# The opening of a two-block kernel redone: c turned first, the first norm's rms taken on token rows, two projections halved over their input rows

## The chip, the cores and the metric

One core of a Trainium2 chip runs the whole program. The metric is device time in microseconds (us); the change is judged against the kernel before. TensorE (PE) multiplies, VectorE (DVE) and ScalarE (ACT) do the elementwise work, GpSimd (POOL) helps, SyncE (SP) issues the weight transfers.

## The reference, cut to what matters

256 tokens of width 1024, f32, pass through two transformer blocks. The change touches only the start of the first:

```python
mod = jax.nn.silu(c) @ w_ada[l] + b_ada[l]              # c: 1 x 1024, w_ada: 1024 x 6144
sh1, sc1, g1, sh2, sc2, g2 = jnp.split(mod[:, None, :], N_MOD, axis=-1)
u = rmsnorm(h, norm1_w[l]) * (1.0 + sc1) + sh1
proj = u @ w_in[l]                                      # 1024 x 3584, seven parts of 512 columns
hq, hf, hi, hg, aq, ak, av = jnp.split(proj, offs, axis=-1)
o_hg = hgrn2(hq, hf, hi, hg, lower_bounds[l], hgrn_gnorm_w[l])   # gated recurrence, uses log of the forget gate of hf
...                                                     # differential attention (aq, ak, av), w_out, norm, FFN
```

Behind it stand the rest of block one, and block two (gated linear attention, retention, 32 experts), which the change leaves as they are.

## The kernel before

**Layout.** Activations are kept with features on the 128 partitions: `hT` is 8 chunks (k = 0 to 7) of 128 features x 256 tokens. x arrives in token rows (`xtok`) and is turned on PE. All small vectors arrive as rows of one tile (`prow`) through 14 transfers, are turned together and copied to `pcol`.

**Gemms.** Each f32 product is made of three fp32r products: x is split into `XH` (ACT) and `XL` (DVE), weights into a high half (ACT, `split_to`, line 872) and a low half (DVE, line 1253), in units of 128 x 1024. A unit of weights gives 24 matmuls of 256 columns (line 520); a projection of 1024 x 512 has four units. There is room for three units (`WHL`), so ACT waits for PE before the fourth. ACT and DVE split two units ahead of the gemm that they stand in.

**Weights.** SP issues pieces of 1 MB in the order of the list `order` into a ring of six slots; a slot is free again when its modulation block was summed (`ada_sum`) or its units were split. The modulation vector is computed in 12 blocks of 512 columns of `w_ada` (2 MB each). Block n gives `modc` columns 4n to 4n+3: blocks 0 and 1 the shift, 2 and 3 the scale of the first norm. A block goes through four engines' steps: `ada_sum` (16 matmuls of 512 columns, line 477), `ada_row` (ACT copy, line 947), `ada_turn` (4 products with `fold`, line 487), `modulation` (DVE, line 1295).

**Opening before.** PE: 16 transposes of x, the transpose of `prow`, the column sums of the squares (`norm_sums`, line 464, on the turned x, squared by ACT), then blocks 0, 1, 2, 3 one after another, 8 spin matmuls, and gemm hf, gemm hq. DVE: reciprocal of `rstd`, normalised x, then per chunk x times scale plus shift and `XL`. Behind gemm hf stands the forget gate: ACT sigmoid, DVE steps (1692 to 1697), ACT Ln (1121), DVE scan (1700). DVE and ACT split no weights in between, beyond the two units ahead. Then a `weave` runs aq, ak, av, hv, hg and wo0 on all engines, with the recurrence (`gated`), blocks 4 to 9 and attention (`diff`) in lanes between gemm steps. Every engine works its instructions in the written order.

Of the kernel before, what the change touches and what calls it, by code (L numbers as in the profile page):

```python
# [14 lines left out]
P = 128  # L15
# [23 lines left out]
            subln=97, gkb=98, glan=102, retn=104, c=120)  # L39
# [55 lines left out]
def build(nc, a, out):  # L95
    ctx = ExitStack()
    with ctx:
# [55 lines left out]
        xtok = early.take([P, TT, D])  # L153
        scratch = Region(ARENA - 1024 - KC * T).take([P, KC, T])
        mrow = [Region(ARENA - 1024 + 512 * i).take([P, 512]) for i in range(2)]
        xmod = Region(P).take([P, KC, T])
# [145 lines left out]
        G = [Gemm("hf", win(1), 0), Gemm("hq", win(0), 0), Gemm("aq", win(4), 0), Gemm("ak", win(5), 0),  # L302
# [49 lines left out]
        order = (["ada0", "ada1", "ada2", "ada3", "hf", "hq", "aq", "ada4", "ada5", "ak", "ada6", "ada7", "av",  # L352
# [30 lines left out]
        def x_last(idx):  # L383
# [17 lines left out]
        S.xT, S.hT_a, S.hT_v = sem("xT"), sem("hT_by_act"), sem("hT_by_dve")  # L401
        S.ada_p, S.ada_a, S.mod, S.xn = (sem(n) for n in ("ada_pe", "ada_act", "ada_mod", "x_normed"))
        S.sqrt_table, S.sq, S.sqw, S.ss, S.rms, S.rstd, S.nrm = (sem("norm_" + n) for n in (
            "table", "squares", "weighed_squares", "sums", "rms", "rstd", "scaled"))
        S.scl, S.lb_v, S.lb_a, S.lam_v, S.lam_a, S.lam_p, S.chain = (sem(n) for n in (
            "scl", "bounds_dve", "bounds_act", "lambda_dve", "lambda_act", "lambda_pe", "chain"))
# [37 lines left out]
        def tensor(e):  # L444
# [24 lines left out]
            def ada_sum(n):  # L469

                b = 6 + n % 2
                clear(b)
                w.wait_ge(S.cT, 1)
                for r in range(2):
                    w.wait_ge(*landed(f"ada{n}", r))
                    for q in range(4):
                        ins = e.matmul(bank[b][32 * q:32 * q + 32, :], c32[:, 4 * r + q, :],
                                       in_slot(f"ada{n}", r, 4, 512)[:, q, :], start=r == 0, stop=r == 1)
                ins.then_inc(S.ada_p, 1)

            def ada_turn(n):

                b = 6 + n % 2
                w.wait_ge(S.consts, 5)
                w.wait_ge(S.ada_a, n + 1)
                for c in range(4):
                    ins = e.matmul(bank[b][:, c:c + 1], mrow[n % 2][:, c * P:(c + 1) * P], fold[:, :], start=True,
                                   stop=True)
                ins.then_inc(S.ada_p, 1)
                free[b] = (S.mod, n + 1)  # L490
# [128 lines left out]
            def third_sums(ks):  # L619
                for k in ks:  # L620
                    for i, x in enumerate((scratch, sq2)):
                        if k == 0:
                            clear(4 + i)
                        w.wait_ge(S.sqw if i else S.sq, k + 1 if i else 2 * KC + k + 1)
# [75 lines left out]
            w.wait_ge(S.d_ident, 16)  # L700
            w.wait_ge(S.d_x, 16)
            for k in range(KC):
                b = 4 + k % 4
                clear(b)
                for j in range(TT):
                    ins = e.transpose(bank[b][:, j * P:(j + 1) * P], xtok[:, j, k * P:(k + 1) * P], ident[:, :])
                ins.then_inc(S.xT, 1)
                free[b] = (S.hT_v if k % 2 else S.hT_a, k // 2 + 1)
            w.wait_ge(S.d_rows, 14 * 16)
            e.transpose(bank[0][:, 0:P], prow, ident[:, :]).then_inc(S.rows_T, 1)  # L710
            free[0] = (S.pcol, 1)
            norm_sums(0)
            for n in range(4):
                ada_sum(n)
                if n == 1:
                    clear(5)
                    w.wait_ge(S.lam_v, 4)
                    e.matmul(bank[5][:, 0:1], ones[0:1, :], lams[0:1, 5:6], start=True, stop=True).then_inc(S.lam_p, 1)
                    free[5] = (S.lam_v, 5)
                ada_turn(n)  # L720
            spin(3, 8)


            run(gemm("hf"))
            run(gemm("hq"))
            weave([gemm(n) for n in ("aq", "ak", "av", "hv", "hg", "wo0")],
                  (0, ada(ada_sum, range(4, 10))),
                  (-1, gated(HG, [(S.hb, 1), by["hq"].freed[1]], by["hv"].freed[1])),
                  (0, ada(ada_turn, range(4, 10))), (4, diff()))
            run(gemm("wo1"))  # L730
            norm_sums(1)
# [129 lines left out]
        def scalar(e):  # L861
# [79 lines left out]
            def norm_split(i, base, shift):  # L941
                for k in range(KC):
                    split_x(base + k, k, scratch[:, k, :], (S.nrm, KC * (i - 1) + k + 1), modc[:, shift + k:shift + k + 1])

            def ada_row(n):
                w.wait_ge(S.ada_p, 2 * n + 1)
                e.activation(mrow[n % 2], bank[6 + n % 2][:, :], ACT.Copy).then_inc(S.ada_a, 1)
# [146 lines left out]
            for dst_, src in row_loads(True):  # L1094
                e.dma_start(dst_, src).then_inc(S.d_rows, 16)
            for k in range(0, KC, 2):
                w.wait_ge(S.xT, k + 1)
                e.activation(hT[:, k, :], bank[4 + k % 4][:, 0:T], ACT.Copy).then_inc(S.hT_a, 1)
            w.wait_ge(S.pcol, 1)
            e.activation(c32[:, :, :], pcol[:, ROWS["c"]:ROWS["c"] + 8].unsqueeze(2).broadcast_to([P, KC, 32]),  # L1100
                         ACT.Silu).then_inc(S.cT, 1)
            norm_rms(0, lambda k: (S.hT_v if k % 2 else S.hT_a, k // 2 + 1))
            ada_row(0)
            w.wait_ge(S.lb_v, 3)
            e.activation(small[:, 20:28], small[:, 20:28], ACT.Exp).then_inc(S.lb_a, 1)
            w.wait_ge(S.lam_v, 2)
            e.activation(lams[:, 2:4], lams[:, 0:2], ACT.Exp).then_inc(S.lam_a, 1)
            for n in range(1, 4):
                ada_row(n)
            w.wait_ge(S.scl, 1)  # L1110
            w.wait_ge(S.xn, 2)
            for k in range(KC):
                e.activation(XH[:, k, :], scratch[:, k, :], ACT.Identity, bias=modc[:, k:k + 1],
                             scale=scl[:, k:k + 1]).then_inc(S.x_hi, 1)
                if k == 0:
                    split_to(2)


            run(gemm("hf", to_features(hf, func=ACT.Sigmoid)))
            w.wait_ge(S.gate_v, 6)  # L1120
            e.activation(hf, hf, ACT.Ln).then_inc(S.gate_a, 1)
            run(gemm("hq", to_features(hq)))
# [7 lines left out]
            norm_rms(1, lambda k: (S.res, k + 1))  # L1130
            norm_split(1, 16, 24)
# [12 lines left out]
            w.wait_ge(S.ss, 3)  # L1144
# [98 lines left out]
        def vector(e):  # L1243
# [38 lines left out]
            def norm_apply(i, base, weight, shift):  # L1282
                w.wait_ge(S.rstd, i + 1)
                w.wait_ge(S.scl, i + 1)
# [8 lines left out]
            def modulation(n):  # L1293
                w.wait_ge(S.ada_p, 2 * n + 2)
                e.tensor_tensor(modc[:, 4 * n:4 * n + 4], bank[6 + n % 2][:, 0:4], pcol[:, 4 * n:4 * n + 4],
                                ALU.add).then_inc(S.mod, 1)
# [340 lines left out]
            w.wait_ge(S.d_lam, 64)  # L1637
            e.tensor_tensor(lamrow[:, 0::2, :], lamrow[:, 0::2, :], lamrow[:, 1::2, :], ALU.mult).then_inc(S.lam_v, 1)
            w.wait_ge(S.lam_v, 1)
            e.tensor_reduce(lams[:, 0:2], lamrow[:, 0::2, :], AXX, ALU.add).then_inc(S.lam_v, 1)  # L1640
            for k in range(1, KC, 2):
                w.wait_ge(S.xT, k + 1)
                e.tensor_copy(hT[:, k, :], bank[4 + k % 4][:, 0:T]).then_inc(S.hT_v, 1)
            w.wait_ge(S.rows_T, 1)
            e.tensor_copy(pcol[:, :], bank[0][:, 0:P]).then_inc(S.pcol, 1)
# [5 lines left out]
            norm_rstd(0)  # L1651
            w.wait_ge(S.rstd, 1)
# [594 lines left out]
```

## Time and profile before

| | us |
|---|---|
| time, median of 3 runs | 1380.79 (1374.78 to 1382.4) |
| the profiled execution, its own time | 1377.91 |
| its span | 1376.1 |
| PE busy | 1290.4 |
| DVE busy | 605.0 |
| ACT busy | 470.5 |

The span is what the profiler saw of the execution; 1.8 us lie around it. PE is the engine that is nearly always at work, so what counts is when it waits, and for whom.

### The profile page before, as it was taken

Reading aid. Unit: us, or ns where it says so; the run is one execution under the profiler, and the core shown is the slowest. Engines: PE = TensorE matmul, PEld = TensorE weight load, DVE = VectorE, ACT = ScalarE, POOL = GpSimd, SP = SyncE. Lnnn points to the kernel's source line nnn. Section 1 sums busy time; section 2 is a strip of 40 time slices with the busy share of each in tenths; the row PEclk is TensorE's granted clock in tenths of the full one; section 3 lists DMA queues with packets and bytes.
Section 4 is the critical chain, followed back from the end, with each engine's and each line's share of the span. In section 5 each row is a group of like instructions: output and inputs, shape, how many; then the busy total and the mean of one; then the engine's idle time right before and its main releaser. Section 6 shows DMA issues by size and latency. Waiting matters only on the chain. (4 is left out here: it accounts for less than half of the span.)

```text
span 1376.1 us, 18603 instructions
## 1 busy us (share of the span) xinstructions
PE 1290.4 (94%) x8067; PEld 958.5 (70%) x8067; DVE 605.0 (44%) x925; ACT 470.5 (34%) x688; POOL 60.9 (4%) x57
## 2 busy tenths in 40 slices
PE   6898869999999999799999999889999999999996
PEld 3886758999998989679999999644344443434432
DVE  2776667344556586485755556431110111101112
ACT  3643545433444644444554454211000000000001
POOL 2021000000000121010020000000000000000000
PEclk9999979999999999899999999999999999999999
DMA  9776313675544434344355545859999999999993
GB/s 353 268 264 241 125 59 123 217 243 184 184 138 153 157 125 161 107 157 150 123 161 185 184 162 179 356 242 401 422 421 421 421 420 421 421 421 421 421 421 136
DMA packets 102163, 349.86 MB, mean 254 GB/s; under 512 B 5856, under 2 KB 9216, under 8 KB 77504
## 3 DMA queue, kind: packets, MB, share of 16 engines
q1 hardware_dynamic: 100624, 345.56, 66.4%
q0 software_dynamic: 1168, 2.99, 0.7%
q8 instruction: 65, 1.06, 0.3%
q14 instruction: 18, 0.15, 0.0%
q10 hardware_dynamic: 288, 0.10, 0.0%
HBM read 347.57 MB, written 1.05 MB: 253 GB/s over the span
## 5 line engine op out<-in xcount | busy, mean ns | idle before, releaser
L520 PE MATMUL bank<-XH,WHL 128*128 128x256 f32 x2928 | 544.2, 286 | 16.2 <-DVE WHL L1253 8.6
L520 PEld LDWEIGHTS bank<-XH,WHL 128*128 128x128 f32 x2928 | 464.6, 194 | 22.9 <-issue 10.7
L520 PE MATMUL bank<-XL,WHL 128*128 128x256 f32 x1464 | 416.5, 285 | 0.0
L1253 DVE TENSOR_TENSOR WHL<-weights,WHL 128x1024 fp32r<-128x1024 f32 x223 | 279.7, 1270 | 209.6 <-ACT WHL L872 209.1
L872 ACT ACTIVATE WHL<-weights 128x1024 fp32r<-128x1024 f32 x223 | 231.8, 1054 | 210.4 <-PE bank L520 210.2
L520 PEld LDWEIGHTS bank<-XL,WHL 128*128 128x128 f32 x1464 | 283.9, 194 | 0.2
L520 PE MATMUL bank<-WHL,XH 128*128 128x512 f32 x320 | 106.0, 406 | 9.4 <-DVE WHL L1253 9.4
L1921 DVE TENSOR_TENSOR chainm<-bank,chainm 128x512 f32<-128x512 f32 x16 | 11.1, 692 | 171.9 <-PE bank L818 171.9
L818 PE MATMUL bank<-weights,arena 128*64 128x512 f32 x384 | 84.5, 592 | 0.0
L818 PE MATMUL bank<-arena 128*64 128x512 f32 x384 | 84.4, 592 | 0.0
L520 PEld LDWEIGHTS bank<-WHL,XH 128*128 128x128 f32 x320 | 62.4, 195 | 26.2 <-DVE WHL L1253 11.7
L1929 DVE COPY yo<-bank 128x512 f32<-128x512 f32 x16 | 11.1, 692 | 144.4 <-PE bank L853 144.4
L818 PEld LDWEIGHTS bank<-arena 128*64 128x64 f32 x384 | 27.6, 137 | 54.8 <-issue 54.8
L818 PEld LDWEIGHTS bank<-weights,arena 128*64 128x64 f32 x384 | 27.5, 137 | 54.6 <-issue 54.6
L520 PE MATMUL bank<-WHL,XL 128*128 128x512 f32 x160 | 64.2, 401 | 0.0
L696 PE MATMUL bank<-yo,arena 128*128 128x512 f32 x128 | 57.7, 593 | 0.8 <-DVE yo L1929 0.8
L683 PE MATMUL bank<-arena 128*128 128x256 f32 x256 | 56.9, 379 | 1.6 <-DVE arena L1615 1.6
L818 PE MATMUL bank<-late_weights,arena 128*64 128x512 f32 x256 | 56.3, 592 | 0.0
L683 PEld LDWEIGHTS bank<-arena 128*128 128x128 f32 x256 | 48.0, 190 | 8.3 <-DVE arena L1615 1.8
L1239 ACT ACTIVATE yo<-bank 128x512 f32<-128x512 f32 x16 | 9.6, 597 | 123.9 <-PE bank L853 123.9
L853 PE MATMUL bank<-arena,masks 128*64 128x512 f32 x192 | 44.5, 614 | 2.7 <-ACT masks L1233 2.7
L853 PE MATMUL bank<-weights,masks 128*64 128x512 f32 x192 | 43.0, 596 | 2.7 <-ACT masks L1233 2.7
(313 smaller groups left out, 1137.6 us busy)
## 6 DMA issues: line engine op xcount, KB each, us to landing
weights<-in_w_in SPq DMA_DIRECT2D x58, 1024.0 KB, 5.0
weights<-in_w_ada SPq DMA_DIRECT2D x24, 1024.0 KB, 7.4
weights<-in_expert_w_gate SPq DMA_DIRECT2D x24, 1024.0 KB, 14.7
weights<-in_expert_w_up SPq DMA_DIRECT2D x24, 1024.0 KB, 16.0
arena<-in_expert_w_up SPq DMA_DIRECT2D x24, 1024.0 KB, 18.5
arena<-in_expert_w_down SPq DMA_DIRECT2D x24, 1024.0 KB, 20.6
weights<-in_expert_w_down SPq DMA_DIRECT2D x24, 1024.0 KB, 21.0
arena<-in_expert_w_gate SPq DMA_DIRECT2D x24, 1024.0 KB, 16.6
```

The costliest lines, as they stand in the source:

```text
L520: ins = e.matmul(o, l, r, start=first, skip_group_check=True, stop=g.part == g.parts - 1 and k == g.kc - 1 and n == 2)
L683: ins = e.matmul(bank[b][:, kk * T:(kk + 1) * T], utok[:, j, k * P:(k + 1) * P], pick[:, j, :], start=j == 0, stop=j == TT - 1)
L696: e.matmul(bank[b][:, :], wpT[p % 2][:, j * P:(j + 1) * P], yo[p % 2][:, n * 512:(n + 1) * 512], start=p == 0, stop=p == NPAIR - 1, skip_g ...
L818: ins = e.matmul(bank[b][64 * s_:64 * s_ + 64, :], xg[:, k, p % 2 * P + 64 * s_:p % 2 * P + 64 * s_ + 64], moe_weights(x, 4, HID)[:, kk, : ...
L853: ins = e.matmul(bank[6 + n][64 * s_:64 * s_ + 64, :], hpT[p % 2][:, k, 64 * s_:64 * s_ + 64], moe_weights(x, 2, D)[:, kk, n * 512:(n + 1) ...
L872: e.activation(unit_halves(U)[0], unit_weights(g, u), ACT.Copy).then_inc(S.w_hi, 1)
L1239: e.activation(yo[p % 2][:, 512:1024], bank[7][:, :], ACT.Copy).then_inc(S.m_ya, 1)
L1253: e.tensor_tensor(lo, unit_weights(g, u), hi, ALU.subtract).then_inc(S.w_lo, 1)
L1921: e.tensor_tensor(hp[p % 2], bank[5][:, :], hp[p % 2], ALU.mult).then_inc(S.m_h2, 1)
L1929: e.tensor_copy(yo[p % 2][:, 0:512], bank[6][:, :]).then_inc(S.m_yv, 1)
```

## The change

1. SP loads c into a tile of its own (`crow`), then x, then b_ada. c is turned alone, first on PE; its silu on ACT no longer waits for `pcol`.
2. Of the other row transfers, two stay on ACT's queue and ten go from ACT's queue to POOL's, behind the four lambda transfers and ahead of `masks`. PE waits for all of them before it turns `prow`.
3. x is turned in four groups of one token block and four chunks; DVE makes all four copies to `hT`.
4. The rms is taken on token rows: ACT squares `xtok` with a sum along the row (2 instructions), square root, DVE reciprocal; DVE multiplies `ident` by it (2 tiles, `diag`), PE multiplies by `ones`, and ACT copies the result to `rstd`. The 8 squares, the column sums and the 128x256 reciprocal go.
5. Modulation blocks come in the order 0, 2, 1, 3. The first two give shift and scale of chunks 0 to 3.
6. hf and hq become hf0, hf1, hq0, hq1, each over half of the input rows (k = 0 to 3, k = 4 to 7, two units each), adding up in the same banks. The order is hf0, hq0 on chunks 0 to 3 (block 1's sum inside hq0, block 3 behind it), then hf1, hq1.
7. Normalising is one DVE instruction per chunk; the shift goes into `XH` and `XL`.

```diff
+        half = lambda name, i, part: Gemm(f"{name}{part}", win(i)[part * 512:(part + 1) * 512, :], 0, kc=4, parts=2, part=part,
+                                          xo=4 * part)
+        G = [half("hf", 1, 0), half("hq", 0, 0), half("hf", 1, 1), half("hq", 0, 1), Gemm("aq", win(4), 0), Gemm("ak", win(5), 0),
...
-        order = (["ada0", "ada1", "ada2", "ada3", "hf", "hq", "aq", "ada4", "ada5", "ak", "ada6", "ada7", "av",
+        ADA = [0, 2, 1] + list(range(3, 12))
+        order = (["ada0", "ada2", "hf0", "hq0", "ada1", "ada3", "hf1", "hq1", "aq", "ada4", "ada5", "ak", "ada6", "ada7", "av",
...
# PE
+            w.wait_ge(S.d_ident, 32)
+            e.transpose(bank[2][:, 0:KC], crow, ident[0:KC, 0:KC]).then_inc(S.rows_T, 1)
...
+            w.wait_ge(S.d_rows, 3 * 16)
+            w.wait_ge(S.d_lam, 14 * 16)
+            e.transpose(bank[0][:, 0:NROWS], prow[0:NROWS, :], ident[0:NROWS, 0:NROWS]).then_inc(S.rows_T, 1)
...
+            for j in range(TT):
+                w.wait_ge(S.x_v, 2 + j)
+                ins = e.matmul(bank[1][:, j * P:(j + 1) * P], ones[:, :], diag[:, j, :], start=True, stop=True)
...
-            norm_sums(0)
-            for n in range(4):
-                ada_sum(n)
...
-            spin(3, 8)
-            run(gemm("hf"))
-            run(gemm("hq"))
+            for i in range(2):
+                ada_sum(i)
+                ada_turn(i)
...
+            spin(0, 4)
+            run(gemm("hf0"))
+            hq0 = gemm("hq0")
+            next(hq0)
+            ada_sum(2)
+            run(hq0)
+            ada_turn(2)
+            ada_sum(3)
+            ada_turn(3)
+            spin(4, 10)
+            run(gemm("hf1"))
+            run(gemm("hq1"))
...
# ACT
+            for j in range(TT):
+                w.wait_ge(S.d_x, 16)
+                e.activation(xsq[:, j, :], xtok[:, j, :], ACT.Square, accum_out=small[:, 44 + j:45 + j]).then_inc(S.x_a, 1)
...
+            def first_split(half):
+                for k in range(4 * half, 4 * half + 4):
+                    split_x(k, k, scratch[:, k, :], (S.nrm, k + 1), modc[:, k:k + 1])
+                    if k == 0:
+                        split_to(2)
+            first_split(0)
+            split_to(4)
+            ada_row(2)
+            ada_row(3)
+            first_split(1)
+            run(gemm("hf1", to_features(hf, func=ACT.Sigmoid)))
...
# DVE
+            def first_norm(half):
+                ks = slice(8 + 4 * half, 12 + 4 * half)
+                w.wait_ge(S.mod, 2 * half + 2)
...
+                for k in range(4 * half, 4 * half + 5):
+                    if k < 4 * half + 4:
...
+                        e.scalar_tensor_tensor(out=scratch[:, k, :], in0=hT[:, k, :], scalar=scl[:, k:k + 1],
+                                               in1=rstd[:, :], op0=ALU.mult, op1=ALU.mult).then_inc(S.nrm, 1)
+                    if k > 4 * half:
+                        split_x(k - 1, k - 1, scratch[:, k - 1, :], modc[:, k - 1:k])
+                        if k == 1:
+                            split_to(1)
+            first_norm(0)
+            split_to(3)
+            w.wait_ge(S.lam_p, 1)
+            e.tensor_copy(neglam, bank[3][:, 0:1]).then_inc(S.lam_v, 1)
+            split_to(4)
+            modulation(2)
+            modulation(3)
+            first_norm(1)
+            run(gemm("hf1"))
...
# POOL, behind the four lambda transfers
+            for dst_, src in row_loads("pool"):
+                e.dma_start(dst_, src).then_inc(S.d_lam, 16)
...
# which queue a row goes to
-                if (name not in ("c", "b_ada")) == on_act:
+                if {"b_ada": "sp", "norm1": "act", "norm2": "act"}.get(name, "pool") == queue:
```

The order on the engines shows what the lists and calls come to. First PE from its start to its first fp32r product, before (L706 turns x, L710 `prow`, L464 the sums of squares, L477 sums and L487 turns a modulation block, L457 spins, L520 is gemm hf):

```order
-L706 MATMUL bank<-ident,arena 128x128 x16
-L710 MATMUL bank<-ident,arena 128x128
-L464 MATMUL bank<-arena,ones 128x256 x8
-L477 MATMUL bank<-weights,c 32x512 x8
-L487 MATMUL bank<-fold,arena 128x1 x4
-L477 MATMUL bank<-weights,c 32x512 x8
-L718 MATMUL bank<-lams,ones 128x1
-L487 MATMUL bank<-fold,arena 128x1 x4
-L477 MATMUL bank<-weights,c 32x512 x8
-L487 MATMUL bank<-fold,arena 128x1 x4
-L477 MATMUL bank<-weights,c 32x512 x8
-L487 MATMUL bank<-fold,arena 128x1 x4
```

And the same place of the change (L709 turns c, L716 x, L722 `prow`, L727 spreads the reciprocal rms, L485 sums and L495 turns a block, L465 spins, L528 is gemm hf0):

```order
+L709 MATMUL bank<-ident,arena 128x8
+L716 MATMUL bank<-ident,arena 128x128 x16
+L722 MATMUL bank<-ident,arena 128x120
+L727 MATMUL bank<-r,ones 128x128 x2
+L485 MATMUL bank<-weights,c 32x512 x8
+L495 MATMUL bank<-fold,arena 128x1 x4
+L485 MATMUL bank<-weights,c 32x512 x8
+L495 MATMUL bank<-fold,arena 128x1 x4
+L734 MATMUL bank<-lams,ones 128x1
+L465 MATMUL bank<-ident 128x128 x4
+L528 MATMUL bank<-XH,WHL 128x256
```

Two blocks instead of four now stand ahead of the first gemm product, and the sums of squares are gone from PE. The second place is DVE from the first block's half to the forget gate, in the change (L1718 normalises a chunk, L1306 writes `XL`, L1284 writes the low half of a unit of weights, L1327 is `modulation`, L1710 `scl`):

```order
+L1284 TENSOR_TENSOR WHL<-weights,WHL 128x1024 x2
+L1727 COPY small<-bank 128x1
+L1284 TENSOR_TENSOR WHL<-weights,WHL 128x1024
+L1327 TENSOR_TENSOR modc<-bank,pcol 128x4 x2
+L1710 SCALAR_TENSOR_TENSOR scl<-modc,pcol 128x4
+L1718 SCALAR_TENSOR_TENSOR arena<-hT,scl,rstd 128x256 x2
+L1306 SCALAR_TENSOR_TENSOR XL<-arena,modc,XH 128x256
+L1718 SCALAR_TENSOR_TENSOR arena<-hT,scl,rstd 128x256
+L1306 SCALAR_TENSOR_TENSOR XL<-arena,modc,XH 128x256
+L1718 SCALAR_TENSOR_TENSOR arena<-hT,scl,rstd 128x256
+L1306 SCALAR_TENSOR_TENSOR XL<-arena,modc,XH 128x256 x2
+L1284 TENSOR_TENSOR WHL<-weights,WHL 128x1024 x4
```

Before, one group of eight chunks stood there with two units of weights split behind the first chunk; now the units of hf1 (the last row) are split behind all four chunks of the second half. The third place is SP's queue, in the change, where pieces of `w_ada` (L2087) and of `w_in` (L2078) now take turns:

```order
+L2067 DMA arena<-in_c 8x128
+L2068 DMA arena<-in_x 128x2x1024
+L2070 DMA arena<-in_b_ada 48x128
+L2087 DMA weights<-in_w_ada 128x4x512 x4
+L2078 DMA weights<-in_w_in 128x4x512 x2
+L2087 DMA weights<-in_w_ada 128x4x512 x4
+L2078 DMA weights<-in_w_in 128x4x512 x4
+L2087 DMA weights<-in_w_ada 128x4x512 x4
```

Before, eight pieces of `w_ada` stood ahead of six of `w_in`; the pieces are as many and as large as before.

## Rows read from the trace of the kernel before

**Rows 1.** Timeline of PE's opening (start, us busy, engine, line, operation, idle before)

```profile
6.84 2.37 PE L706 MATMUL bank<-ident,arena 128*128 128x128 f32 x10 [6.84 <-DMA arena<-in_x]
...
10.86 0.39 PE L710 MATMUL bank<-ident,arena 128*128 128x128 f32 x1
...
14.73 5.23 PE L464 MATMUL bank<-arena,ones 128*128 128x256 f32 x16 [3.49 <-ACT arena L930]
...
19.90 1.92 PE L477 MATMUL bank<-weights,c 128*32 128x512 f32 x16
...
23.58 1.92 PE L477 MATMUL bank<-weights,c 128*32 128x512 f32 x16
...
30.83 1.92 PE L477 MATMUL bank<-weights,c 128*32 128x512 f32 x16
...
33.47 1.05 PE L487 MATMUL bank<-fold,arena 128*128 128x1 f32 x8 [0.72 <-ACT arena L947]
```

**Rows 2.** The same view of PE, DVE and ACT: last modulation block to the first gemm product

```profile
34.38 2.03 PE L457 MATMUL bank<-ident 128*128 128x128 f32 x16
34.56 0.16 DVE L1295 TENSOR_TENSOR modc<-bank,pcol 128x4 f32<-128x4 f32 x1 [3.46 <-PE bank L487]
34.76 0.17 DVE L1674 SCALAR_TENSOR_TENSOR scl<-modc,pcol 128x8 f32<-128x8 f32 x1
34.96 0.60 ACT L1113 ACTIVATE XH<-arena,modc,scl 128x256 fp32r<-128x256 f32 x1 [1.54 <-DVE scl L1674]
...
37.82 0.39 PE L520 MATMUL bank<-XH,WHL 128*128 128x256 f32 x1 [1.40 <-DVE WHL L1253]
```

**Rows 3.** Groups by line and form, 38 to 66 us: splits and the forget gate

```profile
L1253 DVE TENSOR_TENSOR WHL<-weights,WHL 128x1024 fp32r<-128x1024 f32 x9 | 10.6, 1218 | 4.1 <-ACT WHL L872 4.1
L872 ACT ACTIVATE WHL<-weights 128x1024 fp32r<-128x1024 f32 x8 | 8.1, 1047 | 8.7 <-PE bank L520 8.7
L1273 DVE TENSOR_TENSOR XL<-arena,XH 128x256 fp32r<-128x256 f32 x7 | 3.0, 426 | 0.2
```

**Rows 4.** Timeline, gemm hf's end, forget gate and gemm hq

```profile
45.59 0.39 PE L520 MATMUL bank<-XH,WHL 128*128 128x256 f32 x1 [1.27 <-DVE WHL L1253]
...
57.09 0.28 PE L520 MATMUL bank<-XH,WHL 128*128 128x256 f32 x1
58.94 3.47 DVE L1253 TENSOR_TENSOR WHL<-weights,WHL 128x1024 fp32r<-128x1024 f32 x3
60.20 0.39 PE L520 MATMUL bank<-XH,WHL 128*128 128x256 f32 x1 [2.84 <-DVE WHL L1253]
```

**Rows 5.** Timeline of POOL and DVE: the lambda transfers, and who waited

```profile
1.27 0.64 POOL L1983 DMA_DIRECT2D lamrow<-in_diff_lambda_q  x1 [0.82 <-POOLq L2237]
...
2.88 0.48 POOL L1983 DMA_DIRECT2D lamrow<-in_diff_lambda_k  x1
...
8.53 0.28 DVE L1638 TENSOR_TENSOR lamrow<-lamrow 1x128 f32<-1x128 f32 x1 [7.04 <-DMA lamrow<-in_diff_lambda_k]
```

**Rows 6.** DMA issues up to 16 us (KB each, us from issue to landing)

```profile
masks<-in_masks POOLq DMA_DIRECT2D x1, 512.0 KB, 7.1
```

**Rows 7.** Windows: span, busy PE, PEld, DVE, ACT, POOL, PEclk, DMA share, GB/s

```profile
14.00:15.00 1.00, 0.27 (x1) 0.30 (x2) 0.00 (x0) 0.99 (x5) 0.00 (x0) 0.72 1.04 383
17.00:18.00 1.00, 1.00 (x4) 0.82 (x3) 0.00 (x0) 0.00 (x0) 0.00 (x0) 0.57 1.05 385
60.00:61.00 1.00, 0.80 (x6) 0.80 (x7) 1.00 (x2) 0.00 (x0) 0.00 (x0) 1.00 0.00 0
124.00:125.00 1.00, 1.00 (x5) 0.53 (x3) 0.56 (x2) 0.00 (x0) 0.10 (x1) 0.50 1.04 383
```

**Rows 8.** Windows: the forget gate's stretch, and PE behind it

```profile
55.00:60.00 5.00, 2.36 (x20) 2.16 (x18) 3.88 (x3) 3.90 (x4) 0.00 (x0) 1.00 0.12 47
62.00:120.00 58.00, 57.98 (x467) 48.87 (x466) 37.48 (x46) 24.30 (x29) 11.21 (x6) 1.00 0.77 266
```

**Rows 9.** Timeline of PE: the first wait of the attention lane

```profile
123.19 1.25 PE L608 MATMUL bank<-arena 64*128 64x128 f32 x8 [2.92 <-DVE modc L1295]
```

More of the change, by code:

```diff
@@ L1093, in scalar @@
             e.dma_start(ident[:, :], a["ident"]).then_inc(S.d_ident, 16)
-            for dst_, src in row_loads(True):
+            for dst_, src in row_loads("act"):
                 e.dma_start(dst_, src).then_inc(S.d_rows, 16)
[L1096 to L1101, printed above, removed]
@@ L1102, in scalar @@
-            norm_rms(0, lambda k: (S.hT_v if k % 2 else S.hT_a, k // 2 + 1))
+            w.wait_ge(S.rows_T, 1)
+            e.activation(c32[:, :, :], bank[2][:, 0:KC].unsqueeze(2).broadcast_to([P, KC, 32]), ACT.Silu).then_inc(S.cT, 1)
+            w.wait_ge(S.consts, 2)
+            e.activation(small[:, 40:41], epsc[:, 0:1], ACT.Sqrt).then_inc(S.sqrt_table, 1)
+            for j in range(TT):
+                w.wait_ge(S.d_x, 16)
+                e.activation(xsq[:, j, :], xtok[:, j, :], ACT.Square, accum_out=small[:, 44 + j:45 + j]).then_inc(S.x_a, 1)
@@ L1106, in scalar @@
             w.wait_ge(S.lam_v, 2)
[L1107 to L1116, printed above, removed]
@@ L1119, in scalar @@
-            run(gemm("hf", to_features(hf, func=ACT.Sigmoid)))
+            e.activation(lams[:, 2:4], lams[:, 0:2], ACT.Exp).then_inc(S.x_a, 1)
+            ada_row(1)
+            def first_split(half):
[7 more added lines that the diff above has]
+            ada_row(3)
@@ L1668, in vector @@
             e.tensor_scalar(lams[:, 5:6], lams[:, 4:5], -LAMBDA_INIT, None, ALU.add).then_inc(S.lam_v, 1)
-            w.wait_ge(S.lam_p, 1)
-            e.tensor_copy(neglam, bank[5][:, 0:1]).then_inc(S.lam_v, 1)
-            for n in range(1, 4):
-                modulation(n)
-            w.wait_ge(S.mod, 4)
-            e.scalar_tensor_tensor(out=scl[:, 0:8], in0=modc[:, 8:16], scalar=1.0,
-                                   in1=pcol[:, ROWS["norm1"]:ROWS["norm1"] + 8], op0=ALU.add,
-                                   op1=ALU.mult).then_inc(S.scl, 1)
@@ L1677, in vector @@
-            w.wait_ge(S.scl, 1)
-            w.wait_ge(S.xn, 2)
-            for k in range(KC):
-                e.tensor_scalar(xmod[:, k, :], scratch[:, k, :], scl[:, k:k + 1], modc[:, k:k + 1], ALU.mult,
-                                ALU.add).then_inc(S.xn, 1)
-                w.wait_ge(S.xn, 3 + k)
-                split_x(k, k, xmod[:, k, :])
-                if k == 0:
-                    split_to(2)
-            run(gemm("hf"))
-            w.wait_ge(*by["hf"].freed[1])
+            modulation(1)
@@ L1701, in vector @@
                                  ALU.mult, ALU.add).then_inc(S.hb, 1)
-            run(gemm("hq"))
+            run(gemm("hq1"))
             weave([gemm("aq"), gemm("ak"), gemm("av"), gemm("hv"), gemm("hg"), out_of_hgrn()],
-                  (-1, gated(HG, [(S.hb, 1), by["hq"].freed[1]])), (0, ada(range(4, 10))), (4, diff()))
+                  (-1, gated(HG, [(S.hb, 1), by["hq1"].freed[1]])), (0, ada(range(4, 10))), (4, diff()))
             w.wait_ge(S.mod, 10)
@@ L2091, in build, with row_loads @@
         RT_LG, RT_SEL, RT_DPOS, RT_EG, RT_E2 = 1, 22, 25, 29, 30
-        def row_loads(on_act):
+        def row_loads(queue):
             rows = []
```

169 lines of the change are left out of this document (93 added, 76 removed).

## Prediction

> **What bounds the kernel now.** The table of busy times first: PE is busy 1290.4 of 1376.1 us, so only its waits can be won, and the change touches those of the first 66 us. The timeline of PE there shows a start in four parts: transposes of x as soon as x has landed at 6.84, then nothing from 11.25 to 14.73, then 5.23 us of column sums, then four modulation blocks 3.6 us apart, the last one's sum from 30.83 [rows 1]. The first gemm product is at 37.82, 2.86 us behind the first `XH`, because a unit of weights must be split high and low ahead of it [rows 2]. Next the groups by form give the prices of a split: 1.05 us on ACT and 1.22 on DVE for a unit, 0.43 for an `XL` [rows 3]. The timeline around the forget gate shows PE run out of split weights at 57.37 and wait 2.84 us until DVE, back from the scan, has made the next unit [rows 4]. Behind it, from 62 to 120 us, PE has 0.02 us of idle time in 58 [rows 8]: whatever PE has gained or lost when aq begins is carried through that stretch unchanged. DMA is 385 GB/s in the opening and nearly idle (0.12) around the gate [rows 7, 8]; it is no bound by itself.
>
> Three sizes for the sum. A unit is 24 products: from 45.59 to 57.37 there are four, so 2.94 us each. gemm hf therefore ends at 45.59 + 5.88 = 51.47, and the first product that needs a split made behind the scan comes at 60.20, 8.73 us later. In the kernel before, aq begins at 60.20 + 5.88 = 66.08 [rows 4].
>
> **The change, step by step.**
>
> *Until the first sum.* The removed work is the 3.48 us wait and 5.23 us of sums [rows 1]. In its place c is turned while x is still under way, ACT squares two tiles 1024 wide (about 1.05 us each, as a split of that width [rows 3]), and DVE makes two small tiles; that is over by about 12, behind the transposes (x is one issue earlier, about 6.4, and 16 transposes take 3.9: 10.4). What ends last is the row transfers. POOL issues the fourth lambda transfer at 2.88 and DVE gets it at 8.53, 5.65 later; issues are 0.48 to 0.54 apart. Ten more behind it: the last goes out at about 7.8 and lands at 13.5 [rows 5]. Bounds: 12.0 (then the diagonal tiles and the first block's second piece decide) and, with the 7.1 us of `masks` [rows 6], 15. Then 0.39 for `prow` and two f32 products of 128 columns, four passes of 0.13 by the spins (16 passes in 2.03) [rows 1, 2]. The first sum starts at 14.4, not 19.90: 5.5 earlier.
>
> The Trainium skill ("DMA: Bandwidth & Descriptors", Anatomy of one DMA) puts a POOL-issued transfer at a fixed 2.0 us beside its bytes. By that the rows would land at 9.8, the bound of 12.0 would decide, and all that follows would be 1.9 us earlier. The lambda transfers, 0.2 KB each, took 5.65, so the sum goes by the row.
>
> *To the first product.* Second sum 3.68 behind the first (23.58 - 19.90): 18.1. From a block's sum to `scl` 4.10 (30.83 to 34.93): 22.2. One normalising instruction, 0.43 as an `XL`, then 2.86 as before from `XH` to PE: 25.5, against 37.82. Hence a head start of 12.3 us [rows 1 to 3]. hf0's weights are the fifth piece behind x: 6.3 MB with x and 0.5 of masks take 17.7 us at 385 GB/s, from about 3: landed at 21, needed at 23.
>
> *The seam.* Now PE's own order decides. From H = 25.5: unit 0 2.94; a wait of about 0.5, since DVE makes nrm, `XL`, nrm, `XL`, `XL` (5 x 0.43) and a low half (1.22) before unit 1 is there; units 1 and 2 5.88; the sum of block 1 1.92; unit 3 2.94; a turn 1.05: H + 15.2 = 40.7. Block 3 then goes with nothing beside it: 4.10 to `scl` (44.8). DVE's four chunks follow, six instructions of 0.43 up to the last normalised one (47.4), the last `XH` 0.6, and only then ACT splits hf1's first unit, 1.05, DVE its low half, 1.22, with 0.1 between: hf1 starts at 50.4. Before, the `XH` and `XL` of chunks 4 to 7 lay beside hf's products; here 9.7 us of chain lie open. PE has the last block (3.7) and ten spins (2.54) in them, to 46.9, and is idle for some 3.5.
>
> *The gate.* hf1 ends 5.88 later, 56.3. The gate's 8.73 us are as they were, and again exactly two split units (hq1) cover PE: aq starts at 65.0, against 66.08. So of 12.3 us 11.2 are given back: 9.7 in the seam, 3.0 for block 1's sum and turn, which used to stand ahead of the gemm, and 0.5 ahead of unit 1, less some 2 us of waits that hf had among its own units (1.27 before 45.59). Gain 1.1 us.
>
> *The rest.* Pieces of hf1 and hq1 are asked for at about 29 and 32 (their slots come free with hf0 and hq0), block 3 at 20; at 385 GB/s hf1 has landed before 38, needed at 48. `masks` leaves POOL 5 us later and is needed beyond 70. The recurrence's first steps wait for the scan and hq1, both shifted like aq. Those edits cost nothing; the transfer would cost from the point where it is 10 us later.
>
> *The clock.* Behind 3.48 us of idle PE the granted clock fell to half: 0.72 from 14 to 15 and 0.57 from 17 to 18 put the fall at 14.4 to 17.9, about 3.4 us. It was at half again behind 2.92 us of idle time, and at 1.00 behind the 2.84 before 60.20 [rows 1, 4, 7, 9]. A fall costs half its length, 1.7 us, where PE is the path. The one of before lies in the column sums, which go: its price is within the 5.5. The change has two new gaps: about 3.1 us between transposes and rows (10.4 to 13.5), and 3.5 at the seam. The three rows don't tell which of them brings a fall: bounds nothing and 3.4 for both. I take one, 1.7.
>
> The Trainium skill ("TensorE: Matmul & The Clock Gate", The HAM clock gate) has 1.2 GHz as the state of an idle PE and 2.4 GHz as that of a busy one. By that both gaps would bring a fall and the time would be 1.7 us higher, rival (c); the row with 2.84 and no fall shows that not every gap near 3 us does.
>
> *Sum.* 1377.91 - 1.1 + 1.7 = 1378.5 for the profiled execution, which stood 2.9 below the median: 1381.4.
>
> **Rivals.**
> (a) *The head start comes through.* If hf1's splits and block 3 were hidden, 12.3 would arrive at aq: 1368.5. For it: PE is fully busy from there on. Against: the instruction order puts the split of hf1 behind all four chunks, on ACT and on DVE.
> (b) *Slower, by the row transfers on POOL.* Each us past 13.5 shifts the first sum and, by PE's order, everything to aq, one for one. At 7.1 us from issue, as `masks`, it is 1.5 more: 1382.9. It decides for "slower" from a landing at about 19, some 11 us from issue. For it: all ten go by one software queue while 385 GB/s of weights run. Against: 0.2 to 8 KB each, and 5.65 measured in the same opening.
> (c) *Both gaps bring a fall*: 1380.8 - 1.1 + 3.4 = 1383.1.
> (d) *The rows land early*, by 12.0: 1.9 less and, with the first gap then short, no fall there; 1381.4 - 1.9 - 1.7 = 1377.8. For it only that their bytes are few; the 5.65 speaks against it.
>
> **How the numbers follow.** 0.5% is 6.9 us, about what a measurement of this kernel can tell from no change. Forecast, with one fall or none, 0.52; (c) 0.22; (d) 0.1; (a), in full or in good part, 0.08; (b) below the point where it decides 0.03, beyond it 0.05. All but (a) and the last stay within 0.5%; since the medians move too (the runs of before reach 6.0 below theirs and 1.6 above), a little is taken off: same 0.84, faster 0.09, slower 0.07. The range runs from (d) less 2.3 for that scatter, 1375.5, to (b) with both falls, 1384.6, plus as much: 1386.9.
>
> **What would show it.** First modulation sum at 14 to 15 with PE waiting for a row transfer ahead of it; first gemm product at 25 to 26; a PE gap of 3 us before hf1, ended by DVE's split of weights, hf1 at about 50; 2.8 us before aq, aq at 64 to 67; a half clock behind one of the gaps. Wrong if hf1 starts before 46, if the rows land past 17, if PE waits for a DMA at hf0, or if 62 to 120 us shows new waits of PE.

## The result

The change is slower by a little: 1385.0 us median (1381.7 to 1388.1, 14 runs) against 1380.1 for the kernel before (1374.8 to 1382.8, 14 runs). The ratio is 1.0037, interval 1.0025 to 1.005: 5.1 us, inside the half per cent that the forecast called no change, with the interval's upper end on its edge, and 3.6 us above the forecast of 1381.4. Of the executions behind this document one, of the kernel with whole projections, took 4554.8 us; its ratio leaves it out.

The profiled execution took 1386.9 and lies 1.9 above its median, with a span of 1385.0; that of before, with a span of 1376.1, lay below its own. So of the 8.9 us between the two spans some 4 belong to the choice of executions. What the traces show is where they arise. PE's opening in the changed kernel, from the timeline (start, us busy, engine, line, operation, idle before), answers to [rows 1, 2]:

```profile
6.76 3.37 PE L716 MATMUL bank<-ident,arena 128*128 128x128 f32 x16 [3.78 <-DMA arena<-in_x]
...
12.81 0.29 PE L722 MATMUL bank<-ident,arena 120*128 120x120 f32 x1 [2.68 <-DMA arena<-in_ret_norm_w]
...
15.29 1.20 PE L727 MATMUL bank<-r,ones 128*128 128x128 f32 x4 [2.19 <-DVE r L1680]
...
16.42 3.64 PE L485 MATMUL bank<-weights,c 128*32 128x512 f32 x16
...
21.82 1.92 PE L485 MATMUL bank<-weights,c 128*32 128x512 f32 x16
```

The rows are waited for until 12.8, as forecast (13.5). But then PE waits 2.2 us more, for DVE's two diagonal tiles, and the first block's sum takes 3.64 us where it takes 1.92 at the full clock. The tiles, and what POOL did beside them (same view):

```profile
10.95 0.54 POOL L1992 MEMSET arena<- 128x512 f32 x1
11.02 4.19 DVE L1680 TENSOR_SCALAR r<-ident,small 128x128 f32<-128x128 f32 x2
11.41 0.97 POOL L1994 MEMSET arena<- 128x1024 f32 x1
...
14.09 0.97 POOL L1995 MEMSET arena<- 128x1024 f32 x1
15.13 0.27 DVE L1682 COPY pcol<-bank 128x120 f32<-128x120 f32 x1
```

Two products of 128x128 end at 15.2, 0.15 us behind the end of POOL's last memset (15.06). The seam and the gate, answering to [rows 2, 4]:

```profile
29.23 0.58 PE L528 MATMUL bank<-XH,WHL 128*128 128x256 f32 x1 [2.30 <-DVE WHL L1284]
49.59 0.16 DVE L1710 SCALAR_TENSOR_TENSOR scl<-modc,pcol 128x4 f32<-128x4 f32 x1
55.33 0.58 PE L528 MATMUL bank<-XH,WHL 128*128 128x256 f32 x1 [3.63 <-DVE WHL L1284]
72.37 0.38 PE L528 MATMUL bank<-XH,WHL 128*128 128x256 f32 x1 [2.83 <-DVE WHL L1284]
```

hf0 starts at 29.23, 8.6 us ahead of hf before; aq starts at 72.37, 6.3 behind. The granted clock, in windows as in [rows 7] (PEclk is the third column from the end):

```profile
13.00:20.00 7.00, 4.81 (x21) 1.53 (x20) 3.26 (x8) 0.38 (x1) 2.06 (x3) 0.51 1.04 390
27.00:34.00 7.00, 4.77 (x24) 4.77 (x25) 6.12 (x10) 4.23 (x6) 0.00 (x0) 0.53 1.05 386
54.00:61.00 7.00, 5.67 (x27) 5.67 (x28) 3.50 (x3) 2.06 (x4) 0.00 (x0) 0.51 0.59 196
133.00:137.00 4.00, 4.00 (x13) 3.11 (x12) 1.93 (x8) 3.20 (x10) 0.00 (x0) 0.63 0.00 1
```

Three falls to half (1.2 of 2.4 GHz) of nearly 7 us each lie ahead of aq, where before there was one of 3.4. The first and the third begin in or just behind a gap of PE (at 13.1 and 54.1); the one at hf0 begins at 26.8, as the four spins end and before the 2.30 us of gap have passed, behind a stretch of sums and turns with short waits. Behind aq PE is 6.4 us behind when the first attention scores start (129.60 against the 123.19 of [rows 9]) and 9.0 behind at the last ones, since there, too, the clock is low for nearly 7 us at a time. The row from 133 to 137 answers to this one of the kernel before, which lies about as far behind its own first scores (3.8 us against 3.4):

```profile
127.00:131.00 4.00, 4.00 (x19) 3.20 (x18) 2.01 (x7) 3.71 (x10) 0.00 (x0) 0.99 0.00 0
```

Behind that nothing is added: 8.9 at the end, the difference of the spans.

### The profile page after: what moved, and what is told of

It reads as the page before. It is cut to its first block and busy times, and to the rows that moved or that the text cites. A ratio compares the mean times of both kernels' runs of the same rounds, so it can differ in the third digit from the quotient of the medians.

```text
span 1385.0 us, 18590 instructions
## 1 busy us (share of the span) xinstructions
PE 1295.9 (94%) x8068; PEld 963.2 (70%) x8068; DVE 607.2 (44%) x926; ACT 467.3 (34%) x680; POOL 65.9 (5%) x67
## 3 DMA queue, kind: packets, MB, share of 16 engines
q1 hardware_dynamic: 100624, 345.56, 66.1%
## 5 line engine op out<-in xcount | busy, mean ns | idle before, releaser
L528 PE MATMUL bank<-XH,WHL 128*128 128x256 f32 x2928 | 548.3, 288 | 19.2 <-DVE WHL L1284 11.8
L528 PEld LDWEIGHTS bank<-XH,WHL 128*128 128x128 f32 x2928 | 467.9, 195 | 26.5 <-DVE WHL L1284 13.3
L528 PE MATMUL bank<-XL,WHL 128*128 128x256 f32 x1464 | 418.4, 286 | 0.0
L1284 DVE TENSOR_TENSOR WHL<-weights,WHL 128x1024 fp32r<-128x1024 f32 x223 | 279.8, 1271 | 211.6 <-ACT WHL L896 211.2
L528 PEld LDWEIGHTS bank<-XL,WHL 128*128 128x128 f32 x1464 | 285.9, 195 | 0.2
L528 PE MATMUL bank<-WHL,XH 128*128 128x512 f32 x320 | 107.0, 409 | 9.5 <-DVE WHL L1284 9.5
L528 PEld LDWEIGHTS bank<-WHL,XH 128*128 128x128 f32 x320 | 63.1, 197 | 26.9 <-DVE WHL L1284 11.8
L528 PE MATMUL bank<-WHL,XL 128*128 128x512 f32 x160 | 64.8, 405 | 0.0
```

Of the source, the lines that this page charges most:

```text
L528: ins = e.matmul(o, l, r, start=first, skip_group_check=True, stop=g.part == g.parts - 1 and k == g.kc - 1 and n == 2)
L1284: e.tensor_tensor(lo, unit_weights(g, u), hi, ALU.subtract).then_inc(S.w_lo, 1)
```

## The experiments

Where PE stands at four points, in each kernel's profile (us; "hf" is the first gemm product; in kernels with whole projections aq starts two split units, 5.9 us at full clock, behind the wait for the scan), and the ratio to the kernel before with its interval. Each profile is of one execution, the ratio is of 11 to 14 executions, and a profile can lie up to 3.5 us from its kernel's median:

| kernel | first sum | hf | aq | first scores | ratio |
|---|---|---|---|---|---|
| before | 19.90 | 37.82 | 66.1 | 123.2 | 1 |
| the change | 16.42 | 29.23 | 72.4 | 129.6 | 1.0037 (1.0025 to 1.005) |
| memsets late | 14.04 | 26.86 | 70.4 | 127.7 | 1.0021 (1.0007 to 1.0035) |
| seam early | 16.43 | 28.40 | 64.8 | 123.6 | 0.9998 (0.998 to 1.0016) |
| spins | 15.90 | 27.00 | 66.3 | 125.0 | 1.001 (0.9995 to 1.0025) |
| product form | 14.44 | 27.17 | 68.7 | 125.9 | one run, no ratio |
| whole projections | 16.40 | 40.98 | 71 | 128.3 | 1.0008 (0.9994 to 1.0022) |
| all three mends | 13.55 | 29.22 | 64.6 | 123.2 | 0.998 (0.9968 to 0.9991) |
| whole, mended | 13.60 | 38.06 | 68.3 | 125.4 | 1.0022 (1.0009 to 1.0035) |
| rows behind | 12.04 | 27.50 | 62.4 | 122.3 | 0.9996 (0.9985 to 1.0006) |
| few spins | 13.66 | 25.99 | 63.0 | 120.2 | 1.0 (0.999 to 1.001) |
| product form and seam | 13.91 | 26.28 | 62.9 | 121.6 | 0.9981 (0.9969 to 0.9993) |

From aq to the first scores PE needs 57.1 to 57.3 us in the kernel before, the change, memsets late, product form, whole mended and few spins. In seam early, spins, all three mends, rows behind, and product form and seam it needs 58.6 to 59.9: there the granted clock fell to half for 3.4 to 7 us at or just behind the 2.83 us wait at the gate, where the others had no fall (whole projections had one as well, which lies ahead of its aq). So of the lead that the column of aq shows for these five, 1.5 to 2.8 us don't arrive at the first scores.

**POOL's memsets held back.**

```diff
             e.dma_start(distc, a["dist"]).then_inc(S.d_masks, 16)
+            w.wait_ge(S.x_v, 3)
             run(gated(HG, []))
```

> The change with one wait more: POOL starts its zeroing memsets (10.49 to 15.06 in the changed kernel) only when DVE has written the two diagonal tiles. Theory P (the two DVE multiplications of 128x128, 4.1 us each where a product of that size should take 0.2, stand still because POOL's memsets run at the same time): the tiles take under 0.4 us each, PE's wait for them (2.2 us before the two products with ones) goes, the first modulation sum starts at 13.6 to 14.2 instead of 16.42, and the median falls by 2 to 3 us from 1385.0, more if a clock fall gets shorter. Rival Q (the form itself, or its scalar that another engine wrote, is slow): the tiles stay at 4 us and the time at 1385.

Measured: median 1384.1. The timeline of this kernel:

```profile
11.06 0.48 DVE L1680 TENSOR_SCALAR r<-ident,small 128x128 f32<-128x128 f32 x2
11.60 0.53 POOL L1991 MEMSET arena<- 128x512 f32 x1 [1.07 <-DVE r L1680]
...
14.04 3.64 PE L485 MATMUL bank<-weights,c 128*32 128x512 f32 x16
```

The two tiles take 0.48 us together instead of 4.19, the first sum starts 2.4 us earlier, aq 2.0. Theory P holds. In time it is 0.16% of 1380, 2.2 us, by the two ratios; their intervals overlap, so that size is as good as the trace's 2.0 and no better, and the plain medians, 1385.0 and 1384.1, lie only 0.9 apart.

The first sum takes 3.64 us here as in the change, although the clock's column reads 1.00 in every microsecond from 8 to 24 of this profile, where it read 0.51 in the change. So the column doesn't show every stretch in which the same products take twice as long; what slowed them here is not shown.

**The same tiles as a product of two tensors**, memsets where they were.

```diff
-                e.tensor_scalar(diag[:, j, :], ident[:, :], small[:, 44 + j:45 + j], None, ALU.mult)
+                e.tensor_tensor(diag[:, j, :], ident[:, :], small[:, 44 + j:45 + j].broadcast_to([P, P]), ALU.mult)
```

> The change with the two diagonal tiles written by DVE as a product of two tensors (ident times the reciprocal spread along the row) instead of a product with a per-partition scalar; POOL's memsets stay where they are, beside it. If any DVE instruction that reads and writes only SBUF stands still while POOL's memsets run, the tiles stay at about 4 us. If it is the scalar form alone, they take about 0.3 us each, the wait of PE for them (2.2 us) goes as it did with the memsets held back, and the first sum starts at about 14.

Measured: a single run of 1383.3, so no ratio. The timeline of this kernel, where POOL's memsets ran from 10.48 to 15.06:

```profile
11.40 0.97 POOL L1994 MEMSET arena<- 128x1024 f32 x1
...
12.19 0.49 DVE L1680 TENSOR_TENSOR r<-ident,small 128x128 f32<-128x128 f32 x2
12.30 0.97 POOL L1995 MEMSET arena<- 128x1024 f32 x1
```

0.49 us in the middle of the memsets. So it takes both: the product with a per-partition scalar, and POOL at work. The Trainium skill ("SBUF — State Buffer", two separate sides) has DVE and POOL share a pair of ports, which is locked for a whole instruction by DVE's fast two-port modes or by POOL, while a DVE product of two inputs in SBUF contends only with a POOL instruction that reads SBUF, as a memset does not; "VectorE: DVE Perf Modes" gives such a mode to a one-tensor product in f32 and not to one of two tensors. Both runs agree with it in kind. By a lock of one instruction, though, the wait would have been one memset, 0.97; it was 4, over four memsets, each of which starts before the one ahead has ended (11.41, 12.31, 13.20, 14.09).

**The seam: hf1's weights split ahead of block 3.**

```diff
@@ ACT
             ada_row(2)
+            split_to(6)
             ada_row(3)
@@ DVE
             modulation(2)
+            split_to(6)
             modulation(3)
```

> The change with the two units of hf1's weights split ahead of block 3's steps: ACT between its copies of blocks 1 and 3, DVE between the two modulation steps. Theory S (the seam costs because splits stand behind all four chunks): the gap before hf1 shrinks from 3.6 us to about zero, hf1 starts 3 to 4 us earlier against the second scl, the half clock behind the gap goes too, aq starts 4 to 6 us earlier, and the median falls to 1379 to 1381. Rival T (the seam is set by something else, such as hf1's weights landing late or the XL of chunk 4): the gap stays above 2 us and the time within 1 us of 1385.

Measured: median 1379.4. PE at the seam of this kernel:

```profile
47.09 1.05 PE L495 MATMUL bank<-fold,arena 128*128 128x1 f32 x8 [0.72 <-ACT arena L971]
48.00 2.48 PE L465 MATMUL bank<-ident 128*128 128x128 f32 x20
50.27 0.35 PE L528 MATMUL bank<-XH,WHL 128*128 128x256 f32 x1
```

There is no gap any more, hf1 runs at full clock, and aq starts 7.5 us earlier than in the change. Of this 0.8 came with hf0 already, because the first sum took 2.79 us in this profile instead of 3.64, which is not the edit's doing; and 1.5 are lost again behind the gate, so that 6.1 arrive at the first scores. 0.39%, 5.4 us: the largest of the single mends. Theory S holds.

**Spins in the three gaps**, 10 behind the transposes, 14 instead of 4, 24 instead of 10.

```diff
+            spin(3, 10)
             w.wait_ge(S.d_rows, 3 * 16)
...
-            spin(0, 4)
+            spin(0, 14)
...
-            spin(4, 10)
+            spin(4, 24)
```

> The change with more spin matmuls that PE throws away: 10 between the transposes of x and the wait for the rows, 14 instead of 4 ahead of hf0, 24 instead of 10 ahead of hf1. Nothing else moves. Theory C (the falls of the granted clock, at 13.5 to 20, 27 to 34 and 54 to 61 in the changed kernel, are brought by PE's idle gaps and cost about 1.9, 1.5 and 2.8 us on PE's path): at least two of the three falls go, aq starts 3 to 5 us earlier and the median is 1380 to 1382.5. Rival D (the falls lie in time in which PE waits anyway, or come whatever PE does): the falls stay, or aq moves by less than 1.5 us.

Measured: median 1381.1. No matmul was taken away and no wait shortened, yet aq starts 6.1 us earlier. Sums take 1.92 throughout:

```profile
15.90 1.92 PE L485 MATMUL bank<-weights,c 128*32 128x512 f32 x16
...
51.70 0.39 PE L528 MATMUL bank<-XH,WHL 128*128 128x256 f32 x1 [0.51 <-DVE WHL L1285]
```

All three falls are gone. Theory C holds for the trace (6.1 us, above its 3 to 5); the ratio gives 0.27%, 3.7 us. One fall of 3.4 us came in a new place, behind the gate's wait (at 67), where the change had none.

**Halving undone.** Four blocks in the order 0, 2, 1, 3, then whole hf and hq; the splits of ACT and DVE in the same order, everything else of the change kept, 8 spins ahead of hf.

```diff
-        G = [half("hf", 1, 0), half("hq", 0, 0), half("hf", 1, 1), half("hq", 0, 1), Gemm(
+        G = [Gemm("hf", win(1), 0), Gemm("hq", win(0), 0), Gemm(
...
-        order = (["ada0", "ada2", "hf0", "hq0", "ada1", "ada3", "hf1", "hq1", "aq"
+        order = (["ada0", "ada2", "ada1", "ada3", "hf", "hq", "aq"
...
-            for i in range(2):
+            for i in range(4):
                 ada_sum(i)
                 ada_turn(i)
```

> The change with its halving undone: hf and hq whole again behind all four modulation blocks (order 0, 2, 1, 3), c first, rms on rows, rows on POOL, one normalising instruction per chunk kept. By the steps of the prediction with the measured start of 16.42: last sum at 29, scl at 33, gemm hf at 36 to 37, aq at 64 to 66 against 72.37 in the change and 66.08 before. If halving is what loses (theory H), the median is 1377 to 1380, below the change by 5 or more. If the opening's new parts lose and halving wins something (rival), the median is above 1385.

Measured: 1382.9, ratio 1.0008. It beats the change by 0.29% (4.0 us), as theory H has it in sign, but stays above H's band and does not beat the kernel before. hf starts at 41, not 36.5, because in this profile the clock was low from the third block's sum until 3 us into hf (window in the columns of above):

```profile
26.00:43.00 17.00, 15.41 (x73) 9.86 (x66) 5.22 (x12) 4.50 (x7) 0.00 (x0) 0.50 1.05 387
```

**All three mends together**: memsets late, seam early, 9 spins in the first gap and 12 ahead of hf0.

> The change with the three mends together: memsets held behind the tiles, hf1's two units split ahead of block 3's steps, and spins in the two gaps of the opening (9 and 12). Sum of the parts as measured alone: first sum 13.7, gemm hf0 about 24.8, hf1 about 46, aq about 60.3, against 72.37 in the change and 66.08 before. If the parts add (theory: each gap or fall lies on PE's path), the median is 1374 to 1377 and the ratio to before 0.995 to 0.998. Rival: what is won in the opening is lost again behind aq, at the attention lane; then the first attention scores start less than 3 us ahead of the kernel before (123.19).

Measured: median 1376.6, ratio 0.998: faster than the change by 0.57% (7.9 us) and than the kernel before by 0.2% (2.8). The theory that the parts add holds in direction only: alone they gave 2.2, 5.4 and 3.7, 11.3 in all, and aq came at 64.6, not 60.3. Two rows say why; they are of the slowest of this kernel's twelve executions (1380.0), so a typical one may have lost less:

```profile
19.52 1.55 PE L485 MATMUL bank<-weights,c 128*32 128x512 f32 x8 [1.22 <-DMA weights<-in_w_ada]
...
24.08 5.49 PE L465 MATMUL bank<-ident 128*128 128x128 f32 x24
```

With the first sum at 13.6 the second block's second piece is not there: PE waits for the transfer until 19.5. And the clock fell there all the same, to half from 20 to 30.6, so that the 12 spins took 5.49 us instead of some 3.05 (one and a half times the 2.03 of eight, [rows 2]) and stood in hf0's way. As to the rival, the first scores start exactly when they do before (123.2): its sign came, and the 1.5 us that aq was ahead went with the fall behind the gate.

**Whole projections with the mends**, and 3 spins between each sum and its turn.

> hf and hq whole behind four blocks, memsets held back, 9 spins in the first gap and 3 between each block's sum and its turn, so that PE is not left idle in the opening. By the rows: first sum 13.7, three more pitches of 3.65, scl at 28.8, gemm hf at 32, no fall of the clock, aq at 60.3: the same as the mended halves. So halving would be worth nothing either way once the rest is mended (median 1374 to 1377). If the clock falls all the same in the chain of blocks (with whole projections it did, from 26 to 43 us), gemm hf starts past 35 and the time is above 1379.

Measured: 1382.2, ratio 1.0022: the theory fails. Not by the clock, as its alternative had it: hf starts past 35 mainly because every block from the second on now waits for its transfer; a fall from 20 to 24 lies within the second one.

```profile
19.46 1.75 PE L485 MATMUL bank<-weights,c 128*32 128x512 f32 x8 [1.11 <-DMA weights<-in_w_ada]
...
26.00 1.06 PE L485 MATMUL bank<-weights,c 128*32 128x512 f32 x8 [0.91 <-DMA weights<-in_w_ada]
...
31.42 1.06 PE L485 MATMUL bank<-weights,c 128*32 128x512 f32 x8 [1.55 <-DMA weights<-in_w_ada]
```

The fourth block's last piece lands at 31.4. In the kernel before its products begin 0.96 us into the sum of 30.83 [rows 1], at 31.8. So with four blocks ahead of the gemm and the transfers in this order the old opening was within 0.4 us of what 385 GB/s allow, and a quicker norm could not have helped it by more. The ratio agrees: with the mends the whole projections did not get faster (1.0022 against 1.0008, intervals overlapping). Only products that need fewer blocks can start earlier, which is what the halving is for.

**Rows waited for by nobody.** The kernel with three mends, with 5 spins in the first gap, and the rows turned behind the first block's sum.

```diff
             for i in range(2):
                 ada_sum(i)
+                if i == 0:
+                    w.wait_ge(S.d_rows, 3 * 16)
+                    w.wait_ge(S.d_lam, 14 * 16)
+                    e.transpose(bank[0][:, 0:NROWS], prow[0:NROWS, :], ident[0:NROWS, 0:NROWS]).then_inc(S.rows_T, 1)
...
                 ada_turn(i)
```

> As the three mends together, and the transpose of the parameter rows moved behind the first block's sum on PE (5 spins in the first gap), so that the ten rows on POOL's queue, landed at 12.8, are waited for by nobody. If they are what holds the first sum in the mended kernel, it starts at 12.0 to 12.4 instead of 13.7, and everything to aq comes 1.3 to 1.7 us earlier than in the kernel with three mends. If the first block's second piece (about 12) or the tiles hold it as well, it starts at 12.8 or later and the time is the same within 0.5 us.

Measured: the first sum starts at 12.04, so the rows had held it. The ratio, 0.9996, is not below that of the kernel with three mends, although aq starts 2.1 us earlier in the profile (the spins ahead of hf0 took 4.57 us instead of 5.49). In this profile too PE waits for the second block's last piece until 19.56, so 1.5 us earlier at the first sum are nothing at the second:

```profile
19.56 1.62 PE L485 MATMUL bank<-weights,c 128*32 128x512 f32 x8 [0.55 <-DMA weights<-in_w_ada]
```

**Four spins ahead of hf0 instead of twelve.**

> The three mends with 4 spins ahead of hf0 instead of 12 (memsets behind the tiles, early splits at the seam, 9 spins in the first gap). In the kernel with 12 the spins ran at half clock from 24.08 to 29.4 and hf0 started only at 29.22, where its operands were there at about 26.5. If they held it up: hf0 at 26.5 to 27, aq 2 to 3 us earlier than 64.55, ratio to before 0.9955 to 0.9975. If a longer idle gap brings another fall in their place, hf0 starts earlier but runs its units at 5.1 us, aq moves by less than 1 us and the ratio stays at 0.998.

Measured: hf0 at 25.99, earlier by 3.2, but aq at 63.0, by 1.6 only, since hf0's first units ran at half clock; ratio 1.0, so the first theory fails in time. In the profile PE's lead over the kernel before is 3.0 us at the first scores and 0.6 at the last ones (160.02 against 160.61): the falls in the attention lane, of nearly 7 us here, take the rest.

**The product form and the early seam, no further spin.**

> Two mends and no spin more than the change has: the diagonal tiles as a product of two tensors (0.49 us for both, beside POOL's memsets, in the run that had it alone) and the early splits at the seam. First sum 13.7 to 14.4, hf0 at 26 to 27, aq at 62 to 64. If the mended tiles and seam carry the gain, the ratio to before is 0.997 to 0.999, as with the spins; if the spins were needed against falls in the first 30 us, it is 0.9995 or above.

Measured: median 1377.3, ratio 0.9981. The tiles and what decided the first sum:

```profile
10.84 0.49 DVE L1681 TENSOR_TENSOR r<-ident,small 128x128 f32<-128x128 f32 x2
...
12.82 0.30 PE L722 MATMUL bank<-ident,arena 120*128 120x120 f32 x1 [2.81 <-DMA arena<-in_ret_norm_w]
```

As good as the kernel with all mends: two edits, three lines in all, carry the gain, and the added spins were not needed. Against the change it is 0.56%, 7.7 us, which is the 2.2 of the tiles and the 5.4 of the seam.

How much is won against the kernel before is less sure. Four kernels have tiles and seam mended; two are faster than it (0.998, 0.9981) and two are level (0.9996, 1.0), and few spins differs from product form and seam only in how the tiles were mended and in nine spins. So kernels that are nearly the same lie 0.2% apart, which is the size of the gain itself. That the mends win 0.4 to 0.6% against the change is clear of all intervals.

## Why the prediction was right, and where it was not

The class (no change by more than half a per cent) and the range held, the range with some luck: its worst case, late rows with both falls, was 1384.6, and the 1385.0 measured lies within only by the 2.3 us added for scatter. The rows and the seam were as forecast; the cost came from the tiles and the clock. In the profiled execution the sum said 1378.5 and 1386.9 came, 8.4 more: 5.7 of them are there at aq (72.4 against 65.0 and one fall of 1.7), and 2.6 arose behind the first attention scores, where the forecast had nothing. That stretch is unchanged code and took 37.3 to 40.1 us in the twelve profiles by the length of its falls, 37.4 in the one of before and 40.0 in the one of the change; that is taken for scatter. Point by point:

- *The rows on POOL's queue* were forecast for 13.5 and came at 12.8. Rival (b) is out, and so is rival (d) with the fixed 2.0 us that the Trainium skill ("DMA: Bandwidth & Descriptors", Anatomy of one DMA) gives a POOL transfer: issued at 7.82, the last one took 5.0.
- *"That is over by about 12"* was wrong: the step on the diagonal tiles failed. They ended at 15.2, because a product with a scalar stood still beside POOL's memsets. I had moved POOL's memsets 5 us later with `masks` in the text, and costed the delay at nothing without asking what they would then lie beside. The first sum came 2.0 us later than forecast by it, although the rows were 0.7 early; the run that took it away won 2.4 there and 2.0 at aq.
- *The seam* was sized right: 5.6 us from `scl` to hf1 forecast, 5.6 measured (49.75 to 55.33), a gap of 3.6 against 3.5. It was the main reason why a head start of 8.6 us was lost, and the early split shows it.
- *The gate* was right to 0.01: a wait of 2.83.
- *The clock* was the term that was mis-sized: one fall of 3.4 us at 1.7 forecast; three of nearly 7 came. Against the forecast's stretches the traces put 1.7 on the first sum, 1.2 between hf0 and hf1 (26.1 against 24.9, although the half microsecond of wait that was forecast ahead of unit 1 did not come) and 2.4 from hf1 to aq (17.0 against 14.6). With the 2.0 of the tiles that is 7.3 on the 65.0 forecast for aq, which gives 72.3, and 72.4 was measured. The forecast counted two new gaps; a third, 2.30 us ahead of hf0 with four spins in place of eight, is not in it and had a fall too. The gap ahead of hf1 (3.6) came with a fall, as the Trainium skill ("TensorE: Matmul & The Clock Gate", The HAM clock gate) would have it, and so did the first; the 2.83 ahead of aq had none here and one of 3.4 to 7 us in six of the other kernels, so neither that page nor the length of a gap near 3 us decides it. The spins, which took the falls away and nothing else, gave 6.1 at aq.
- *Rival (a)* did not come, and *(c)*, two falls, was the nearest: one fall more, and each twice as long.
- *"It is no bound by itself"*, of DMA, held in the change, but only because the tiles and the clock made PE late; once these were mended, the second block's transfer was what PE waited for.

That halving as written costs 4 us is shown by a pair of runs (1.0037 against 1.0008), and so is that it wins 3 to 6 us once tiles and seam are mended (0.998 to 1.0 against 1.0022 with whole projections). Against the kernel before the mended halving is 0 to 0.2% ahead by its four ratios. The mends add up to 11.3 us alone and 7.9 together, and it is the spins that don't add: tiles and seam give 2.2 and 5.4 alone and 7.7 together, the spins 3.7 alone and nothing beyond. That fits with falls that come with gaps, so that closing the gap at the seam and filling it win the same microseconds, and with the transfer that is next; which of the two takes how much wasn't taken apart. Left open is what sets the length of a fall: the same place of the attention lane had 3.4 us in some profiles and nearly 7 in others, and that is as large as the effects sought here.

## What to carry to other kernels

When a dependent chain is cut in two so that its first half can start early, look at what the second half now waits for: work that lay beside products before (here a split of weights behind four chunks) lies open at the seam, unless it is moved ahead of the wait. Ask of a faster opening which transfer it will meet next; here 8 MB of blocks left 0.4 us to win with whole projections. And when one queue's work is moved later, look at what it will run beside.

## What the runs showed of the hardware

- Two f32 products of 128x128 with a per-partition scalar, SBUF to SBUF, took 4.19 us on DVE while POOL wrote four memsets of 128x1024 in a row, 0.48 without them; the product of two tensors took 0.49 beside such memsets.
- Idle gaps of PE of 2.3 to 3.6 us went with half the clock for nearly 7 us in the change, where the kernel before had 3.4 with a gap of 3.5. The same wait of 2.83 us at the gate had no fall with it in six profiles and one of 3.4 to 7 us in the other six. Chains of sums with short waits between had the clock low for 17 us in one profile, for 4 in another and not at all in the kernel before.
- The granted clock's column can read 1.00 where products take twice as long: the first sum, 1.92 us at best, took 3.64 with the column at 0.51 in the change and 3.64 with it at 1.00 in the kernel with late memsets.
- Twelve spin products took 5.49 us at half the clock, and eight took 2.03 at full clock, which makes some 3.05 for twelve: cover that is counted in instructions becomes a delay when the clock falls.
